# Expert rows in four column quarters, transposed on VectorE, and expert weights in loads of 32 partitions

## The reference

```python
u = rms_norm(x, norm2_g) * (1.0 + sc2) + sh2      # sc2, sh2, g2: columns of the conditioning
aff = softmax(u @ w_router)                       # 16 experts in 4 groups
# best group by the sum of its two best affinities, then the best two experts in it
gate = normalised affinities of these two, 0 for the others
for e in range(16):
    h = silu(u @ w1[e]) * (u @ w3[e])             # (512, 1024) @ (1024, 512)
    y = y + gate[:, e:e+1] * (h @ w2[e])          # (512, 512) @ (512, 1024)
x = x + g2 * y
```

## Time and profile before

| | |
|---|---|
| median of 3 runs | 776.78 us |
| the profiled execution | 775.59 us |
| its span, first to last instruction | 773.9 us |
| mean granted clock of TensorE | 0.912 |
| TensorE matmul / VectorE / ScalarE busy | 627.6 / 325.6 / 253.9 us |
| DMA traffic | 176.25 MB, 155.02 read from HBM |
| expert stage (first block to last output block) | about 444 to 745 us |

### The profile page before, as it was taken

The page is one execution under the profiler, slowest core; times in us unless marked ns, Lnnn a source line. Parts: engine busy times, 40 slices in busy tenths (PEclk is TensorE's granted clock), DMA queues, the critical chain, the costliest instruction groups (busy, mean ns, idle before and its releaser), DMA issues.

```text
span 773.9 us, 15587 instructions
## 1 busy us (share of the span) xinstructions
PE 627.6 (81%) x6210; PEld 375.8 (49%) x6211; DVE 325.6 (42%) x925; ACT 253.9 (33%) x611; POOL 79.6 (10%) x118
## 2 busy tenths in 40 slices
PE   0898999967689888889975088989999999999940
PEld 0544464744456556554455054545555555555520
DVE  4704827251586779933453122222222222222215
ACT  4200200141365547821240033333444334433410
POOL 5001000043100000000000400101110011101122
PEclk9998999989598999999985589999999999999985
DMA  8970947070898000056053549999999999999228
GB/s 334 378 273 27 407 164 272 0 228 0 287 278 224 2 1 1 3 187 248 0 188 139 224 133 320 365 357 366 367 366 366 365 365 363 370 367 359 59 58 300
DMA packets 81388, 176.25 MB, mean 228 GB/s; under 512 B 9410, under 2 KB 26378, under 8 KB 79306
## 3 DMA queue, kind: packets, MB, share of 16 engines
q1 hardware_dynamic: 68592, 152.90, 56.5%
q0 software_dynamic: 8384, 13.97, 5.3%
q10 hardware_dynamic: 4380, 8.94, 3.6%
HBM read 155.02 MB, written 20.71 MB: 227 GB/s over the span
## 4 chain that ended last, share of the span: by engine, by line
PE 27%; DMA 23%; DVE 2%; issue 2%; POOL 2%; ACTq 0%; ACT 0%; POOLq 0%
DMA featT<-expert_rows 21%; PE score L1534 9%; PE score L1454 7%; PE score L1543 4%; PE bank L1524 4%; PE score L1494 2%; DMA pool_sb<-expert_rows,idx 1%; POOL expert_rows L768 1%; POOL pool_sb L788 1%; DMA expert_rows<-pool_sb,idx 1%; DMA expert_rows<-featT 1%; PE bank L1549 0%; ACTq L664 0%; PE bank L1486 0%; PE bank L1402 0%
## 5 line engine op out<-in xcount | busy, mean ns | idle before, releaser
L1534 PE MATMUL score<-pool_sb,featT 128*32 128x256 f32 x2688 | 162.6, 386 | 21.0 <-DMA featT<-expert_rows 12.2
L1534 PEld LDWEIGHTS score<-pool_sb,featT 128*32 128x32 f32 x2688 | 86.8, 111 | 82.9 <-DMA featT<-expert_rows 26.7
L1250 PE MATMUL bank<-pool_sb,featT 128*128 128x512 f32 (+2 forms) x256 | 89.3, 511 | 5.8 <-DVE featT L843 2.6
L1190 DVE TENSOR_TENSOR featT<-featT,score 128x128 f32<-128x128 f32 x42 | 12.1, 287 | 185.3 <-ACT featT L675 185.3
L1543 PE MATMUL score<-pool_sb,featT 128*32 128x256 f32 x1344 | 83.5, 390 | 0.4 <-ACT featT L680 0.4
L1250 PEld LDWEIGHTS bank<-pool_sb,featT 128*128 128x128 f32 x256 | 50.1, 197 | 43.4 <-issue 35.5
L669 ACT ACTIVATE featT<-bank,mod_col 128x32 f32<-128x32 f32 x129 | 39.4, 375 | 61.1 <-PE bank L1524 61.1
L776 POOL DMA_DIRECT2D expert_rows<-featT x42 | 29.2, 694 | 279.6 <-DVE featT L1186 266.0
L1180 DVE TENSOR_SCALAR featT<-bank,mod_col 128x32 f32<-128x32 f32 x215 | 50.9, 302 | 14.9 <-PE bank L1524 14.9
L1454 PE MATMUL score<-pool_sb,featT 128*128 128x512 f32 x128 | 55.6, 594 | 0.0
L675 ACT ACT_TABLE_LOAD x42 | 53.9, 1283 | 0.8
(11 more groups left out here) (243 smaller groups left out, 685.7 us busy)
## 6 DMA issues: line engine op xcount, KB each, us to landing
pool_sb<-in_moe_w SPq DMA_DIRECT2D x48, 2048.0 KB, 20.9
pool_sb<-in_ada_w SPq DMA_DIRECT2D x16, 1024.0 KB, 6.9
expert_rows<-zeros_f SPq DMA_DIRECT2D x17, 512.0 KB, 6.7
featT<-expert_rows ACTq DMA_DIRECT2D x44, 128.0 KB, 5.4
expert_rows<-featT POOLq DMA_DIRECT2D x42, 128.0 KB, 7.1
pool_sb<-in_ada_w SPq DMA_DIRECT2D x8, 640.0 KB, 11.1
pool_sb<-in_w_out SPq DMA_DIRECT2D x4, 1024.0 KB, 17.0
pool_sb<-in_ada_w SPq DMA_DIRECT2D x8, 384.0 KB, 9.7
```

Of the source, the lines that this page charges most:

```text
L1250: m = nc.tensor.matmul(pj_bank(g, i)[:, 0:n], featT[:, k, i * P:(i + 1) * P], w_stage[:, g % 3, k, 0:n], start=(k == 0), stop=(k == KD - 1))
L1534: mm = nc.tensor.matmul(banks[0][h * BT:(h + 1) * BT, 0:2 * HB], xgT[:, k, :], exp_w13[slot][:, :, k, h * HB:(h + 1) * HB], start=(k == 0) ...
```

## The change

- A fetch now brings the 32 rows in four column quarters: `xg[n]` is 128 partitions x 256 columns, where partition 32 h + r holds columns h * 256 to (h + 1) * 256 of row r. There are two such buffers.
- VectorE applies scale and shift to the rows (`rows_in`: two operations of 128x256, with `scale2_part` and `shift2_part`, which hold the quarters of the two vectors for all partitions) into `xm`, and transposes `xm` in squares of 32x32 (`xg_T`): partition 32 h + a of piece k now holds column h * 256 + k * 32 + a. The hidden rows are transposed in the same manner (`hmid_T`). TensorE's transposes and their evacuations on VectorE and ScalarE go.
- Since a partition now holds other columns of the rows, it needs other rows of the weights: "(h k a) n -> h a k n". Each 2 MB matrix is loaded in four DMAs of 512 KB, one for each quarter of 32 partitions, in the order 0, 2, 1, 3. The runs stay at 2 KB for w1 and w3 and 4 KB for w2. The semaphores count four times as much.
- ScalarE fetches block g + 3 at the head of block g, when the first operation of `rows_in(g + 1)` has released the buffer; silu is its only other work in the loop.
- TensorE's order per block is inner(g), outer(g - 1).
- Early in the kernel SyncE loads norm2_g, spread over the partitions (four small DMAs), and TensorE and VectorE make the two new vectors with `quarters`.

The diff, without the declarations of semaphores and of the two vectors:

```diff
...
@@ -178,13 +180,20 @@
         blkbuf = featT[:, :, :].rearrange("p k n -> p (k n)")
-        xg = blkbuf[0:BT, 0:D]
-        xgT = blkbuf[:, D:D + KD * BT].rearrange("p (k n) -> p k n", k=KD)
-        silu = blkbuf[:, 2 * D:2 * D + HB]
-        hmid = blkbuf[:, 2 * D + HB:2 * D + 2 * HB]
-        hT = blkbuf[:, 2 * D + 2 * HB:2 * D + 2 * HB + P]
-        y_sb = [blkbuf[:, 3 * D + n * DN:3 * D + (n + 1) * DN] for n in range(2)]
-        y_last = [blkbuf[:, 3 * D + (2 + n) * DN:3 * D + (3 + n) * DN] for n in range(2)]
+        blk_at = [0]
+
+        def blk_view(n):
+            blk_at[0] += n
+            return blkbuf[:, blk_at[0] - n:blk_at[0]]
+
+        xg = [blk_view(DN) for _ in range(2)]
+        xm = blk_view(DN)
+        xgT = blk_view(DN).rearrange("p (k r) -> p k r", r=BT)
+        silu = blk_view(HB)
+        hmid = blk_view(HB)
+        hT = blk_view(HB).rearrange("p (k r) -> p k r", r=BT)
+        y_sb = [blk_view(DN) for _ in range(2)]
+        y_last = [blk_view(DN) for _ in range(2)]
 
@@ -408,6 +417,8 @@
                 sp.dma_start(vrow[28:32, b * DH:(b + 1) * DH], beta_swa[0, half].rearrange("(i d) -> i d", d=DH)).then_inc(s_small, 16)
+            for h in range(NT):
+                sp.dma_start(scale2_part[h * BT:(h + 1) * BT, :], norm2_g[0:1, h * DN:(h + 1) * DN].broadcast_to([BT, DN])).then_inc(s_n2, 16)
             for n, pos in enumerate((cmp_pos_k, cmp_pos_v)):
@@ -447,8 +458,9 @@
                 done = e_w2[e % 3] if m == 2 else e_w13[e % 3]
-                sp.dma_start(chunk_of(e % 3, m, DE // P if m == 2 else KD),
-                             MOE_W[m][0, e].rearrange("(k p) n -> p k n", p=P)).then_inc(done, 16)
+                to, of = chunk_of(e % 3, m, DE // P if m == 2 else KD), MOE_W[m][0, e].rearrange("(h k a) n -> h a k n", h=NT, a=BT)
+                for h in (0, 2, 1, 3):
+                    sp.dma_start(to[h * BT:(h + 1) * BT], of[h]).then_inc(done, 16)
 
@@ -460,7 +472,8 @@
             load_matrix(2, 2)
-            sp.wait_ge(s_xg, 32)
+            sp.wait_ge(s_xg[0], 16)
+            sp.wait_ge(s_xg[1], 16)
             load_matrix(2, 0)
@@ -660,35 +673,27 @@
 
-            def xg_load(g):
-                act.dma_start(xg, xs[bass.ds(g * BT, BT), :]).then_inc(s_xg, 16)
-
-            def xg_T(g):
-
-                for k in range(3):
-                    m = nc.scalar.activation(xgT[:, 5 + k, :], banks[5][:, k * BT:(k + 1) * BT], ACT.Identity,
-                                             scale=mod_col[:, 21 + k:22 + k], bias=mod_col[:, 29 + k:30 + k])
-                m.then_inc(m_xa, 1)
-
-            def block_of_rows(g):
+            def xg_load(g, n):
+                act.dma_start(xg[n], xs[bass.ds(g * BT, BT), :].rearrange("r (h n) -> h r n", h=NT)).then_inc(s_xg[n], 16)
+
+            def block_of_rows(g, n):
+                act.wait_ge(m_sc, g + 2)
+                xg_load(g + 3, 1 - n)
                 act.wait_ge(m_h1, g + 1)
                 nc.scalar.activation(silu, banks[0][:, 0:HB], ACT.Silu).then_inc(m_si, 1)
-                act.wait_ge(m_xt, g + 2)
-                xg_load(g + 2)
-                xg_T(g + 1)
-                act.wait_ge(m_ht, g + 1)
-                nc.scalar.activation(hT, banks[6][:, 0:P], ACT.Copy).then_inc(m_hT, 1)
 
             act.wait_ge(s_scat, 16 * 2 * TT)
-            xg_load(0)
-            act.wait_ge(m_xt, 1)
-            xg_load(1)
-            xg_T(0)
+            xg_load(0, 0)
+            xg_load(1, 1)
+            act.wait_ge(m_sc, 1)
+            xg_load(2, 0)
             act.wait_ge(t_gs, 1)
-            total = all_blocks(act)
-            with act.Fori(0, total) as g:
-                block_of_rows(g)
-            act.wait_ge(s_xg, total * 16 + 32)
+            pairs = block_pairs(act)
+            with act.Fori(0, pairs) as m:
+                for n in range(2):
+                    block_of_rows(m * 2 + n, n)
+            act.wait_ge(s_xg[0], pairs * 16 + 32)
+            act.wait_ge(s_xg[1], pairs * 16 + 16)
             nc.scalar.activation(ssq2, ssq2, ACT.Copy)
@@ -876,13 +881,14 @@
                                 nc.vector.tensor_copy(gate1_row[:, 512:1024], banks[1][:])
+                                nc.vector.tensor_copy(shift2_part[:], banks[3][:, 0:DN])
                                 nc.vector.tensor_copy(mod_col[:, 24:32], banks[2][:, 0:8]).then_inc(s_modc, 1)
...
                                 dve.wait_ge(s_mod, 4)
-                                for h in range(NT):
-                                    at0 = (h * DN) % 512
-                                    nc.vector.tensor_copy(gate2_part[h * BT:(h + 1) * BT, :],
-                                                          banks[h * DN // 512][h * BT:(h + 1) * BT, at0:at0 + DN])
+                                nc.vector.tensor_copy(gate2_part[:], banks[0][:, 0:DN])
+                                dve.wait_ge(s_n2, 16 * NT)
+                                nc.vector.scalar_tensor_tensor(out=scale2_part[:], in0=banks[1][:, 0:DN], scalar=1.0, in1=scale2_part[:],
+                                                               op0=ALU.add, op1=ALU.mult)
                                 nc.vector.scalar_tensor_tensor(
@@ -1174,41 +1180,66 @@
 
+            def rows_in(g, n):
+                dve.wait_ge(s_xg[n], g * 8 + (16 if n == 0 else 8))
+                if not (isinstance(g, int) and g == 0):
+                    dve.wait_ge(m_xT, g)
+                nc.vector.tensor_tensor(xm, xg[n], scale2_part[:], ALU.mult).then_inc(m_sc, 1)
+                dve.wait_ge(m_sc, g + 1)
+                nc.vector.tensor_tensor(xm, xm, shift2_part[:], ALU.add).then_inc(m_mod, 1)
+
             def xg_T(g):
-                dve.wait_ge(m_xt, g + 1)
-                for k in range(5):
-                    m = nc.vector.tensor_scalar(xgT[:, k, :], banks[4][:, k * BT:(k + 1) * BT], mod_col[:, 16 + k:17 + k],
-                                                mod_col[:, 24 + k:25 + k], ALU.mult, ALU.add)
-                m.then_inc(m_xv, 1)
-
-            def rows_out(y, upto):
-                dve.wait_ge(m_y, upto)
+                dve.wait_ge(m_mod, g + 1)
+                nc.vector.transpose(xgT, xm.rearrange("p (k r) -> p k r", k=KD)).then_inc(m_xT, 1)
+
+            def hmid_T(g):
+                dve.wait_ge(m_h, g + 1)
+                nc.vector.transpose(hT, hmid.rearrange("p (k r) -> p k r", k=NT)).then_inc(m_hT, 1)
+
+            def rows_out(y):
                 nc.vector.tensor_tensor(y, banks[2][:, 0:DN], gate2_part[:], ALU.mult).then_inc(m_ye, 1)
 
-            def block_of_rows(g):
+            def hidden(g):
+                dve.wait_ge(m_h1, g + 1)
+                xg_T(g + 1)
                 dve.wait_ge(m_si, g + 1)
+                if not (isinstance(g, int) and g == 0):
+                    dve.wait_ge(m_hT, g)
                 nc.vector.tensor_tensor(hmid, silu, banks[0][:, HB:2 * HB], ALU.mult).then_inc(m_h, 1)
-                xg_T(g + 1)
+
+            def block_of_rows(g, n, y):
+                hidden(g)
+                dve.wait_ge(m_y, g)
+                hmid_T(g)
+                rows_out(y)
+                rows_in(g + 2, n)
 
             nc.vector.memset(y_last[0][0:1, 0:1], 0.0).then_inc(m_ye, 1)
+            rows_in(0, 0)
             xg_T(0)
-            block_of_rows(0)
+            rows_in(1, 1)
+            hidden(0)
+            hmid_T(0)
+            rows_in(2, 0)
             dve.wait_ge(t_gs, 1)
...
             for g in range(1, 3):
-                block_of_rows(g)
-                rows_out(y_sb[(g - 1) % 2], g)
+                block_of_rows(g, g % 2, y_sb[(g - 1) % 2])
             with dve.Fori(1, pairs - 1) as m:
-                block_of_rows(m * 2 + 1)
-                dve.wait_ge(s_ys[0], m * 16)
-                rows_out(y_sb[0], m * 2 + 1)
-                block_of_rows(m * 2 + 2)
-                dve.wait_ge(s_ys[1], m * 16)
-                rows_out(y_sb[1], m * 2 + 2)
-            block_of_rows(pairs * 2 - 1)
+                for n in range(2):
+                    hidden(m * 2 + 1 + n)
+                    dve.wait_ge(m_y, m * 2 + 1 + n)
+                    hmid_T(m * 2 + 1 + n)
+                    dve.wait_ge(s_ys[n], m * 16)
+                    rows_out(y_sb[n])
+                    rows_in(m * 2 + 3 + n, 1 - n)
             last = dve.value_load(block_start[0:1, NE + 2:NE + 3], min_val=MIN_BLOCKS * NE - 1, max_val=MAXB)
-            rows_out(y_last[0], last)
-            rows_out(y_last[1], last + 1)
+            hidden(last)
+            dve.wait_ge(m_y, last)
+            hmid_T(last)
+            rows_out(y_last[0])
+            dve.wait_ge(m_y, last + 1)
+            rows_out(y_last[1])
 
@@ -1292,8 +1323,19 @@
                     row, col = (0, 1024) if g == 2 else (1024, 0)
-                    for h in range(2):
-                        nc.tensor.matmul(banks[h][:], ones[:], acc[:, b, row + h * 512:row + (h + 1) * 512], start=True, stop=True)
+
+                    def quarters(to, at0):
```

(55 more changed lines are left out.)

## The result

The changed kernel takes 951.78 us, the median of 4 runs (947.82 to 952.47), beside 777.19 us for the kernel before: ratio 1.2238, 95% interval 1.2201 to 1.2274. The forecast was 910 us, with a range of 775 to 955.

A forecast was written before the change was run, and what follows sets the result against it. Block loop and expert weight stream nearly tied before; afterwards the stream at 213 GB/s bounds: 462 + 384 + 20 = 866 us, + 13 = 879, + 29.1 = 908, + 1.7 = 910 us. Range 775 to 955.

The forecast's parts named there:

- The stretch of w_out: Earlier load of w_out in 64-partition pieces, 213 GB/s with busy engines; taken as the rate of the new expert weight loads.
- The start of the stream: Expert stage: after expert 0's three blocks, the remaining 39 weight matrices were to start streaming near 462 us.
- The head of the kernel: Early kernel: four more small loads, a copy and four small matmuls were to add 1 us.
- I take 20: Expert stage: 39 blocks of row traffic were to add 20 us to 384 us of weights, from 0 to 48 or more.
- a landing above 6 us: Expert stage: sign that would show the new row fetch running on only four engines.
- The tail: After the last matrix: an outer product and two blocks, 13 us, then 29.1 us for the rest as before.
- 2.3 us per block: Expert stage: VectorE's work per block, below TensorE's 5.52 us, so zero on the path.
- The table load of ScalarE: Expert stage: the change was to remove it, leaving no table load per block.
- Rival 1: Expert stage: paired engines drift into opposite halves, so weights stream at full 365 GB/s; 758 us, chance 0.13.
- Rival 2: Expert stage: weights at full rate, but the row fetch on four engines; 803 us, chance 0.12.
- Rival 3: Expert stage: engine pairs drift apart over hundreds of microseconds, mean 260 GB/s; 841 us, chance 0.07.
- Rival 4: Expert stage: the row fetch is not freed, up to 6.7 plus 2.1 us, under two blocks; no chance of its own.

The follow-up runs named there:

- experiment 1: The kernel before, with only each weight load cut into four loads of 32 partitions (order 0, 2, 1, 3): 913.02 us, ratio 1.1721.
- experiment 5: The changed kernel with consecutive weight rows per partition, strided VectorE transposes, and each matrix in four 512 KB loads over all 128 partitions: 789.73 us, ratio 1.0189.
- experiment 3: The changed kernel with consecutive weight rows per partition and strided VectorE transposes, each matrix still in four loads of 32 partitions: 1001.51 us, ratio 1.2899.
- Experiment 6: Row fetch split into four DMAs, in three kernels: the changed kernel 896.77 us, that of experiment 5 750.56 us, that of experiment 2 770.01 us.
- experiment 7: The changed kernel with the fetch in four DMAs: quarters in order 0, 1, 2, 3, 922.07 us; or each quarter cut into four 128 KB loads, 837.89 us.
- experiment 2: The changed kernel with consecutive weight rows per partition, one load per matrix onto 128 partitions, and strided VectorE transposes: 823.89 us, ratio 1.0606.

## Why the prediction was right, and where it was off

**The weight stream.** Right, and shown. The stretch of w_out foretold the rate: 213 GB/s there, 205 to 220 in the changed kernel. In the kernel before, the cut alone takes the expert stage from 365 to 236 GB/s, and the weights by themselves from 395 to 224 (experiment 1). With the weights in place, as many loads of the same size give 337 GB/s onto 128 partitions and 194 onto 32 (experiments 5 and 3). Part of that gap is the late fetch of the latter, but where no fetch is in flight, from 345 to 360 us, it is 410 against 224. The rule of the Trainium skill, "SBUF — State Buffer", section "Door 1: The DMA port swizzle", that 64 partitions from 0 on are no better than 32, is borne out here: 189 GB/s for halves and 194 for quarters, or 210 and 224 with only weights in flight. Which ports are shared no run here shows; a half of the speed, and its dependence on the alternation of halves, are what was measured.

**The start of the stream.** 462 us forecast, 466 measured. The terms of the forecast themselves, 446.2 + 5.8 + 2 x 5.52, give 463; the prediction wrote 462. The head of the kernel was costed at 1 us and took 4: the output projection starts at 340.9 us in place of 336.9. 2.2 us of it stand at 112 us, where TensorE resumes the input projections at 116.59 and not at 114.43 us: the four small matmuls and the copy of 128x256, at 0.41 us, come before it in a chain. The rest was not followed up.

**The price of the row traffic.** This is the term that was mis-sized. "I take 20" was put on 384 us for the weights; the stream took 441, thus 57 us by that division (and 69 if the weights are put at the 220 GB/s that they reach alone), above the 48 us for all bytes at 213 GB/s. The upper end of the range, 955, was worked out with 65. The other errors cancel by luck: 910 + 4 for the start + 37 here - 3 for the tail - 1 behind it is 947, and the profiled execution took 947.8 us. Experiment 6 shows what the term was: with the fetch on all engines the time falls by 48 to 64 us. The prediction had the mechanism (32 pieces of 1 KB on each of four engines, 1.5 us a block), but weighed it down, on the ground that an engine that waits for its half has time to spare. It has not: a load is complete only when its slowest engine is, and the others run dry (share 0.95 in place of 1.07). The first fetches of the changed kernel, with nothing else in flight, show the few engines directly, 446 to 449 us in 40 slices:

```profile
DMA  0000000000000031011112222323232322111222
```

One to three tenths busy, as four of 16 engines would be, where the old fetch had 0.8 to 0.9. The sign that the prediction named for this, a landing above 6 us, can't be read: the profile gives no landing times for these fetches. By the rule of the Trainium skill on the number of engines, "DMA: Bandwidth & Descriptors", section "Why a DMA increments its semaphore by 16 and not by 1", the slowest dimension of 4 gives four: the trace agrees, now for ScalarE's DMAs as well.

**The tail.** 13 us forecast from the last matrix to the last output block, 10.4 measured (907.7 to 918.1 us): behind the last matrix stand three outer products and one inner one (1.9 and 3.6 us), where the forecast counted two inner ones. Then 28.1 us follow in place of 29.1.

**VectorE and the blocks.** 2.3 us per block forecast; the timeline's six operations sum to 0.45 + 0.25 + 0.31 + 0.39 + 0.41 + 0.42 = 2.23 us. It is hardly on the path: TensorE waits for its product six times, 11.1 us in all, before 513 us, thus before the weights are late for the first time. The table load of ScalarE was expected to vanish; 21 of 42 remain, at no cost.

**The rivals.** Rival 1, full rate, did not happen: 205 to 209 GB/s. Its cause may still be real, as experiment 7 shows a gain that grows with the changes of half. Rival 2, full rate with the fetch on four engines, was put at 803 us; experiment 5 is that kernel but for its longer runs and took 790. Rival 1's time was 758 us; the version with 2 KB runs, whole-width loads and the fetch on all engines took 760. So these sums came close for kernels that the change was not, in part by luck: that version moves 378 GB/s, and the sum took 365. Rival 3, a slow drift to 260 GB/s, is not seen in the changed kernel; in experiment 1 the rate does rise, from 236 GB/s (500 to 740 us) to 252 (785 to 845 us), and why was not followed up. Rival 4, that the fetch stays in the way, was given no chance: nearly true at packets of 2 and 4 KB, where TensorE waits 11.1 us (changed kernel) and 13.0 us (experiment 5) for VectorE's product, but not at 16 KB (experiment 2), where it waits 89.4 us, and 32 pieces in a row behind packets of 0.59 us are 19 us by an estimate from these figures.

## What to carry to other kernels

Look for a partial-width load in the trace before cutting a wide one: with the same busy share, half the GB/s. A new data layout need not cost the full-width load: give each partition consecutive rows, and let the transposing engine read with a stride; here this and the fetch on all engines turned a loss of 22% into a gain of 3.8%. And see to it that a small transfer with a short outermost dimension does not sit on a few engines of a stream that is the bound: here this cost about as much as its packets took on these, 59 us by the prediction's estimate, 48 to 64 us measured.

## What the runs showed of the hardware

- Loads onto 32 or 64 partitions keep the DMA engines as busy as loads onto 128, and move 0.51 to 0.57 of the bytes: 395 and 224 GB/s from 345 to 360 us in the same kernel, 410, 224 and 210 with the weights in place.
- The delay of a small fetch beside a stream grows with the stream's packets, as if the two took turns by packets. With the fetch on all engines it lands in a median of 5.3 us beside weight packets of 4 KB, and in 8.5 us beside packets of 16 KB.
- Contiguous runs of 2, 4 and 16 KB travelled in packets of about that size. Runs of 4 KB gave 389 GB/s and of 2 KB 378 in the same kernel (more loads for 2 KB), and 16 KB gave nothing more (385, at a share of 1.00 against 1.04).
- Loads of 256 to 512 KB were no worse than loads of 2 MB in a full stream: 378 GB/s in runs of 2 KB, where the kernel before, with its other fetch, has 365.
